# Two heads ahead in an attention stage, its convolution taps moved elsewhere, and the merge's remainders given to GpSimd

## The reference

```python
proj = rms_norm(x, g_mix) @ w_in            # split into the inputs of four branches and their gates
y_a = dsa_attention(qa, ka, va, qi, ki, iw) @ w_oa          # 4 heads of 128, top 64 keys by index scores
u   = causal_dwconv(glu_a * sigmoid(glu_b), cb_conv_w, cb_conv_b)      # 31 taps, 512 channels
y_b = silu(layer_norm(u)) @ w_ob
y_c = (gb * causal_dwconv(gc * xc, cc_conv_w)) @ w_oc        # 3 taps
y_d = stick_breaking_attention(sq, sk, sv) @ w_od
merged = g0 * y_a + g1 * y_b + g2 * y_c + g3 * y_d           # gates: sigmoid(gate_in + b_gate)
x = x + merged @ w_merge
h2 = rms_norm(x, g_ffn)
x = x + (silu(causal_dwconv(h2 @ w_gate)) * (h2 @ w_up)) @ w_down
```

## Time and profile before

| | |
|---|---|
| median of 3 runs | 2931.35 us (2930.52 to 2932.72) |
| profiled execution | 2930.85 us, span 2929.1 us |
| TensorE busy | 2791.6 us, 95% |
| VectorE busy | 1955.8 us, 67% |
| ScalarE busy | 1176.6 us, 40% |
| GpSimd busy | 535.0 us, 18% |
| mean granted TensorE clock | 0.987 |

### The profile page before, as it was taken

How to read it: one execution, slowest core, us unless ns; L and a number is a source line. 1 busy time by engine, 2 the same in 40 slices (tenths; PEclk the granted TensorE clock), 3 DMA queues, 4 the chain that set the end, 5 groups by cost and what they waited for, 6 DMA issues and landing times.

```text
span 2929.1 us, 43506 instructions
## 1 busy us (share of the span) xinstructions
PE 2791.6 (95%) x18162; PEld 2512.1 (86%) x18162; DVE 1955.8 (67%) x2817; ACT 1176.6 (40%) x1564; POOL 535.0 (18%) x408
## 2 busy tenths in 40 slices
PE   4999999989999999999999999999989999999999
PEld 3888888857888888888877999998989999998999
DVE  3767854385767857557467755887666778867665
ACT  4222244375312143121456434445544444445443
POOL 0200100000100101001000100896000129920000
PEclk8999999999999999999999999999999999999999
DMA  7546532202546545354322475553456665535565
GB/s 254 178 149 201 181 98 87 87 1 72 156 155 200 180 129 154 119 160 151 124 72 59 141 198 155 163 173 117 150 166 179 164 180 154 158 109 182 158 182 140
DMA packets 593171, 427.37 MB, mean 146 GB/s; under 512 B 16848, under 2 KB 571088, under 8 KB 592720
## 3 DMA queue, kind: packets, MB, share of 16 engines
q1 hardware_dynamic: 592976, 424.59, 48.9%
HBM read 423.50 MB, written 1.05 MB: 145 GB/s over the span
## 4 chain that ended last, share of the span: by engine, by line
PE 81%; DVE 10%; ACT 5%; DMA 2%; issue 2%; SPq 0%; ACTq 0%; DVEq 0%
PE ps L715 23%; PE ps L716 23%; PE ps L717 23%; DVE w_lo L1806 4%; ACT w_hi L1262 3%; PE ps L939 1%; PE ps L940 1%; PE ps L941 1%; PE ps L815 1%; PE ps L816 1%; PE ps L817 1%; PE pm L918 1%; DMA raw<-in_w_in 1%; DVE tap_t L2606 1%; PE ps L1073 1%
## 5 line engine op out<-in xcount | busy, mean ns | idle before, releaser
L715 PE MATMUL ps<-h_hi,w_hi 128*128 128x256 f32 (+1 forms) x3616 | 1156.8, 320 | 40.9 <-DVE h_lo L1930 24.1
L716 PE MATMUL ps<-h_lo,w_hi 128*128 128x256 f32 (+1 forms) x3616 | 1146.6, 317 | 0.0
L717 PE MATMUL ps<-h_hi,w_lo 128*128 128x256 f32 (+1 forms) x3616 | 1146.1, 317 | 0.0
L1806 DVE TENSOR_TENSOR w_lo<-raw,w_hi 128x2048 fp32r<-128x2048 f32 (+2 forms) x376 | 811.2, 2158 | 308.8 <-ACT w_hi L1262 305.2
L1262 ACT CAST w_hi<-raw 128x2048 fp32r<-128x2048 f32 (+2 forms) x376 | 631.1, 1679 | 439.9 <-PE ps L717 298.0
L715 PEld LDWEIGHTS ps<-h_hi,w_hi 128*128 128x128 f32 x3616 | 695.8, 192 | 92.9 <-issue 27.7
L716 PEld LDWEIGHTS ps<-h_lo,w_hi 128*128 128x128 f32 x3616 | 696.0, 192 | 43.3 <-issue 0.2
L717 PEld LDWEIGHTS ps<-h_hi,w_lo 128*128 128x128 f32 x3616 | 695.8, 192 | 43.2
L2630 POOL TENSOR_TENSOR act_lo<-sil,act_hi 128x512 fp32r<-128x512 f32 (+1 forms) x132 | 159.8, 1211 | 1722.7 <-DVE act_hi L2050 1331.9
L715 PE MATMUL ps<-act_hi,w_hi 128*128 128x256 f32 (+1 forms) x1122 | 367.8, 328 | 1.9 <-DVE w_lo L1806 1.7
L716 PE MATMUL ps<-act_lo,w_hi 128*128 128x256 f32 (+1 forms) x1122 | 366.5, 327 | 0.0
(11 more groups left out here) (289 smaller groups left out, 3023.9 us busy)
## 6 DMA issues: line engine op xcount, KB each, us to landing
chunk_w<-in_ada_t SPq DMA_DIRECT2D x128, 512.0 KB, 3.4
raw<-in_w_in SPq DMA_DIRECT2D x62, 1024.0 KB, 5.4
raw<-in_ffn_pre_wi SPq DMA_DIRECT2D x88, 512.0 KB, 5.2
raw<-in_ffn_post_wi SPq DMA_DIRECT2D x88, 512.0 KB, 5.2
raw<-in_ffn_pre_wo SPq DMA_DIRECT2D x32, 704.0 KB, 4.5
raw<-in_ffn_post_wo SPq DMA_DIRECT2D x32, 704.0 KB, 4.7
raw<-in_w_ffn_gate SPq DMA_DIRECT2D x44, 512.0 KB, 4.0
raw<-in_w_ffn_up SPq DMA_DIRECT2D x44, 512.0 KB, 5.3
```

What stands on the lines that cost most here:

```text
L715: pe.matmul(o, hi, x_hi[:, k, tok], start=k == 0, stop=False)
L716: pe.matmul(o, hi, x_lo[:, k, tok], start=False, stop=False)
L717: return pe.matmul(o, weights(w_lo[u.low], u, k, m * P, P), x_hi[:, k, tok], start=False, stop=k == u.run.kc - 1)
L1806: nc.vector.tensor_tensor(w_lo[u.low][:, 0:n], whole[:, 0:n], w_hi[u.slot][:, 0:n].bitcast(F32), ALU.subtract).then_inc(lo_ready, 1)
```

## The change

Three things change.

1. In `soft`, TensorE's `turn(1)` and `scores(3)` come before the second half of unit 1, and units 2 and 3 are computed whole. VectorE's queue is rewritten to suit: `normed(1)` comes ahead of the first split, `normed(2)` and `chunk_out(0)` ahead of the second, and only two taps stand in the stage. ScalarE takes `copied(2)` ahead of `gate(2)`.
2. The taps: `glu` takes 8 in place of 6, the values 1 in place of 2, `soft` 2 in place of 4, and so the ob gates 8 in place of 7.
3. The merge: the remainders `h_lo` are computed on GpSimd in a new stage function `merge`, no longer on VectorE by `merged_lo`; VectorE's last split follows its last `add_branch` at once.

```diff
-        for st, per, at_most in ((g, 3, 6), (c, 2, 12), (v, 1, 2), (a, 1, 4), (ob_gates, 4, CB_TAPS)):
+        for st, per, at_most in ((g, 4, 8), (c, 2, 12), (v, 1, 1), (a, 1, 2), (ob_gates, 4, CB_TAPS)):
...
 (TensorE, soft)
                 weigh(0)
-                beside(s, 1, 1)
                 turn(1)
                 scores(3)
-                beside(s, 2, 0)
+                beside(s, 1, 1)
+                turn(2)
                 weigh(1)
-                beside(s, 2, 1)
-                turn(2)
-                beside(s, 3, 0)
+                whole_beside(s, 2)
+                turn(3)
                 weigh(2)
-                turn(3)
-                beside(s, 3, 1)
+                whole_beside(s, 3)
                 weigh(3)
...
 (ScalarE, soft)
                 split_ahead(s.beside[2][1])
+                copied(2)
                 gate(2)
-                copied(2)
                 split_ahead(s.beside[3][1])
...
 (VectorE, soft)
                 normed(0)
-                split_ahead(s.beside[0][1])
-                conv_taps(s, 0)
                 masked(2)
                 maximum(2)
                 negative(2)
                 reciprocal(1)
                 normed(1)
+                split_ahead(s.beside[0][1])
+                reciprocal(2)
+                normed(2)
+                chunk_out(0)
                 split_ahead(s.beside[1][1])
-                conv_taps(s, 1)
-                chunk_out(0)
                 masked(3)
                 maximum(3)
                 negative(3)
-                reciprocal(2)
-                normed(2)
-                split_ahead(s.beside[2][1])
-                conv_taps(s, 2)
-                chunk_out(1)
+                conv_taps(s, 0)
                 reciprocal(3)
                 normed(3)
+                chunk_out(1)
+                split_ahead(s.beside[2][1])
+                conv_taps(s, 1)
+                chunk_out(2)
                 split_ahead(s.beside[3][1])
-                conv_taps(s, 3)
-                chunk_out(2)
                 chunk_out(3)
...
 (VectorE, branch_out)
-                    if s.next is not None and u.j:
-                        merged_lo(s.next, u.j - 1)
-
                 sweep(dve, s.run, weigh)
                 if s.next is not None:
-                    merged_lo(s.next, s.run.n - 1)
                     split_ahead(Unit(s.run, s.run.n - 1))
...
 (GpSimd)
+            def merge(s):
+
+                for c in range(KC):
+                    pool.wait_ge(S["m_hi"], s.b["m_hi"] + c + 1)
+                    rest(h_lo[:, c, 0:SEQ], merged[:, c, :], h_hi[:, c, 0:SEQ], "m_lo")
```

More of the change, by code:

```diff
@@ L2182, in diff @@
                     head_out(i)
[L2184 to L2188, removed]
             def angle_steps(j):
@@ L2716, in stick @@
                         mask(z_e[:, h % 2, :], z_e[:, h % 2, :], NEG, "z_arg_m")
-            todo = dict(ffn_in=act_lows, conv_in=act_lows, diff=diff, glu=glu, cc=cc, stick=stick, layernorm=layernorm)
+            todo = dict(ffn_in=act_lows, conv_in=act_lows, diff=diff, glu=glu, cc=cc, stick=stick, layernorm=layernorm, merge=merge)
             for s in stages:
```

## The result

The changed kernel takes 2938.64 us (median of 20 runs, 2932.84 to 2943.28), the kernel before 2932.28 (20 runs on the same chips, 2928.18 to 2936.09). The ratio is 1.0023, 95% interval 1.0017 to 1.0029: 0.2% slower, some 6.7 us by the ratio and 6.4 between the medians, where 5.1 us less were forecast, and the time lies 7.8 above the end of the range.

What follows compares the result with a forecast made beforehand. TensorE, busy for 95% of the span, was taken as the bound. `soft` +4.9, column sums -0.35 and merge +0.6 gave 5.1 us won: 2931.35 - 5.1 = 2926.3 us, range 2923.0 to 2930.8.

Steps and rivals of the forecast that it cites:

- the term of +0.6: Merge: the second unit begins 0.3 us earlier with GpSimd's remainders at the median time, 0.6 us won in two layers.
- rival 2: Merge: GpSimd's remainders take 1.59 us each, so only 1.3 us is won in all, 2930.0 us; chance 0.10.
- +4.9: `soft`: old waits and low clock go, a new wait comes; 2.1 us won in layer 0, 2.8 in layer 1.
- 1.1 stood: `soft`: `weigh(1)` would wait 1.1 us in each layer for ScalarE's `copied(1)`, queued behind `gate(1)`.
- ready by 2001.2 at worst, in time: `soft`, layer 0: VectorE's `normed(1)`, given 0.8 to 1.7 us, would be done before `turn(1)` at 2001.5.
- Rival 5: `soft`: VectorE is late for `turn(3)` or `turn(1)`, 1.5 us a layer; 2.1 us won, 2929.2 us; chance 0.05.
- rival 1: Merge and column sums: remainders and split run undisturbed, sums do not wait; 6.9 us won, 2924.5 us; chance 0.22.
- 0.35 stood: Ob gates, layer 0: two more taps delay TensorE's column sums, 0.35 us lost; nothing in layer 1.
- rival 4: `glu`: taps of 0.9 us or more make splits late and TensorE wait; up to 2939.9 us; chance 0.05.
- GpSimd's taps start 0.8 later: `glu`: its last `cb_in` stands behind two added taps; GpSimd ends `cc` at 2019.6, still before `stick` needs it.
- rival 3: Clock: both waits now are followed by low clock, 1.54 us each; 2.0 us won, 2929.3 us; chance 0.10.
- 1.54 us each time: `soft`, layer 1: low clock after the wait of `turn(2)` cost 1.54 us, taken as the price of a spell.

Runs made afterwards that it cites:

- part 3 alone: The kernel before with only the merge's remainders moved to GpSimd: 2941.10 us, ratio 1.0030.
- the copy ahead of the gate: The changed kernel with the merge's remainders back on VectorE, and `copied(1)` ahead of `gate(1)` in ScalarE's queue: 2926.51 us, ratio 0.9978 to the kernel before.
- the one with the added wait: The kernel before with the merge's remainders on GpSimd, and VectorE's last split waiting until GpSimd has finished them: 2931.72 us, ratio 1.0001.
- the kernel without part 3: The changed kernel with the merge's remainders back on VectorE: 2928.21 us, ratio 0.9989 to the kernel before.
- the new order with the old `glu`: The kernel before with the change's order of `soft`, two taps there, nine beside the ob gates, `glu` and values as before: 2930.75 us, ratio 0.9999.
- the taps alone: The kernel before with only the taps moved as in the change: 2924.92 us, ratio 0.9979.
- four lines: ScalarE's rounding of merged pairs one step later, first on the changed kernel with VectorE remainders, `copied(1)` ahead, seven ob-gate taps: 2917.48 us, ratio 0.9957 to the kernel before.

## Why the prediction was wrong

**The step that failed is the merge**, the term of +0.6. It read "the nearest row for GpSimd's is `ob_lo`" and took that row's median, 0.96 us, and as the worst case its longest, 1.59. Beside VectorE's split the two remainders that decide take 2.60 and 2.76 us. `ob_lo` was no bound: the traces show a GpSimd subtraction held for what is left of VectorE's instruction, and a split of 128 x 2048 lasts 2.29 us. The bound from the rows would have been one split and its own 0.73, 3.0 us, with two such in a row. I also let the split start earlier, and took that as a gain; it is what puts the two side by side. The second merge unit was to come 0.3 us closer to the first and comes 3.6 and 3.2 later. From the first merge unit to the norm part 3 costs 4.6 us in each layer of the profile, where +0.3 was booked; some 3.2 of it stand without low clock behind (layer 0 of part 3 alone), and the rest comes with the low clock. Between the medians part 3 alone costs 9.3 us.

The Trainium skill says in SBUF — State Buffer, Who interferes with whom, that the port pair which VectorE and GpSimd share is an exclusive lock: a VectorE instruction with two SBUF inputs and a GpSimd instruction that reads SBUF block each other, and the one that issues second waits for the whole of the first. The trace agrees, in both directions: the remainder is over 0.58 us after the split, the next split 2.15 after the remainder. The page of the Trainium skill that the prediction weighed tells of contention without saying how much, and so rival 2 had the right sign and 1.6 us a layer where 4.6 came.

**Soft**, +4.9, gave 2.6. The waits of `turn(2)` and `turn(3)` went, 3.23 and 2.33 us, the clock stayed at 1.00, and `weigh(1)` waits 0.97 where 1.1 stood: right, and the copy ahead of the gate confirms the cause. Wrong was "ready by 2001.2 at worst, in time": `normed(1)` was given 1.7 us with its reciprocal by the longest row of `normed(2)`, and took 2.80 alone. It is the same error as in the merge, since a row's longest value is no worst case where two queues can meet anywhere. With GpSimd's addition elsewhere the order gave 4.8, so the size was right for that order and wrong for this combination. Rival 5 named `turn(1)`; rival 1, that nothing disturbs anything, fell with both terms.

**The taps** were costed by their own time alone. The column sums wait 0.26 where 0.35 stood, layer 1 not at all, and `glu` bears the two taps a unit, so rival 4 fell. But I wrote "GpSimd's taps start 0.8 later", which is so and more (5.76 us between the last two `cb_in` for 4.96, and GpSimd's first tap 1.2 later by the stamps of `glu`), and looked only at GpSimd's end for it, not at which of VectorE's instructions its additions would then meet. That shift is worth -4.4 us in the old `soft` (69.11 against 73.56, fewer taps in both) and +2.2 in the new one (70.49 against 68.24).

**The clock**, rival 3: low clock behind the merge's wait for its first weights did come, in both layers of the changed kernel and also where VectorE keeps the remainders. The prediction went by one trace that lacks it. Of the eleven kernels here that have this wait of 3.1 us, eight show low clock behind it in both layers, part 3 alone in one, and only the kernel before and the one with the added wait in none. Its price was wrong as well: not 1.54 us each time. In the changed kernel (0.82 over the first unit) it costs nothing, since TensorE waits for the remainders behind it, in the kernel without part 3 (0.77) 0.1, and only in that of the new order with the old `glu` (0.64) as much as 1.24. The costly one is the other, at the start of the second unit; it stands in five of the six layers in which remainders and splits collide and in none of the others.

What stays open: 2 us of what the taps alone win; what decides whether low clock comes behind the first weights' wait; and why the addition moves by 2.2 us when GpSimd starts 1.2 later. The shift is whole when GpSimd begins `cc` (180.24 us after `glu`'s first matmul for 177.74), so it grows before `soft`. That the new order moves the addition by 1.9 fits a VectorE split that no longer stands ahead of it: in the two kernels that differ by the order alone, GpSimd's four products take 5.64 us beside that split and 3.73 without.

## What to carry to other kernels

Before work is given to GpSimd, look at what VectorE does at that moment, not at how long GpSimd's instruction takes on the whole: where both read from SBUF as these do, cost it at the rest of VectorE's instruction plus its own, and if it is on TensorE's path, put a wait between them or leave it where it is. A change of a few instructions on an engine that feeds GpSimd moves GpSimd's long instructions against VectorE's short ones 150 us of schedule later, so tune such parts together and test them apart. And look at the waits next to the change: those of 3.06 us at the first merge unit, 6.1 in two layers, are more than the 5.1 that I had forecast of the whole change, and fell to 0.6 to 0.8 each with four lines.

## What was not expected of the hardware

VectorE's TENSOR_SCALAR, with one operand in SBUF besides its column of scalars, is held by GpSimd's addition as well: the pair of `normed(1)` took 2.80 and 2.83 us beside one, and 0.67 beside a small one. Even an instruction of 128 x 2 elements took 1.94 us so, in the changed kernel, and ended with the addition (2016.73 and 2016.70):

```profile
2014.79 1.94 DVE L2235 TENSOR_SCALAR stats<-stats 128x2 f32<-128x2 f32 x1
...
2014.31 2.39 POOL L2649 TENSOR_TENSOR cc_sum<-cc_sum,cc_product 128x1024 f32<-128x1024 f32 x1
```

An engine's total busy time hides this: GpSimd's remainders have a median of 0.74 us in the changed kernel, and the few of up to 2.77 are the ones that TensorE waits for.
